# One ring of 1 MB weight units and fp32r products for the mixers of an eight-stage decoder kernel

## The chip, the cores and the metric

The kernel runs on one core of a Trainium2 chip. Its engines are TensorE (PE: matmuls; its weight loads are shown apart, as PEld), VectorE (DVE), ScalarE (ACT), GpSimd (POOL) and SyncE (SP), whose queue issues the weight loads. Each engine works through its own instructions in order and waits on semaphores. The metric is device time in microseconds, the median of several executions. One further execution is profiled; all rows come from that one.

## The reference, cut to what matters

256 tokens of width 1024 in float32 go through two blocks of two layers each: four mixers, three feed-forward networks, and a mixture of experts at the end.

```python
def first_block(x, ...):                      # layer 0: attention_mixer, layer 1: recurrent_mixer
    for layer in range(DEPTH):
        h = rmsnorm(x, norm_mix_pre[layer])
        m = attention_mixer(h, ...) if layer % 2 == 0 else recurrent_mixer(h, ...)
        x = x + rmsnorm(m, norm_mix_post[layer])
        h = rmsnorm(x, norm_ffn_pre[layer])
        f = swiglu(h, ffn_w_gate[layer], ffn_w_up[layer], ffn_w_down[layer])
        x = x + rmsnorm(f, norm_ffn_post[layer])

def second_block(x, ...):
    h = x + dilated_diff_mixer(rms_norm(x, attn_norm), attn_w_in, ..., attn_w_out)
    h = h + swiglu_2(rms_norm(h, ffn_norm), ffn_w_gate, ffn_w_up, ffn_w_down)
    h = h + hgrn2_mixer(rms_norm(h, hgrn_norm), hgrn_w_in, ..., hgrn_w_out)
    return h + moe_swiglu(rms_norm(h, moe_norm), moe_w_router, moe_w_gate, moe_w_up, moe_w_down)

def recurrent_mixer(h, w_in, conv_w, conv_b, w_a, b_a, w_i, b_i, lam, w_out):
    gate, xr = jnp.split(h @ w_in, 2, axis=-1)
    gate = jax.nn.gelu(gate, approximate=True)
    xc = causal_conv(xr, conv_w) + conv_b     # 4 taps, then blocks of 256 columns
    r = jax.nn.sigmoid(blocks(xc) @ w_a + b_a)
    i = jax.nn.sigmoid(blocks(xc) @ w_i + b_i)
    log_a = -LRU_C * r * jax.nn.softplus(-lam)
    a, u = jnp.exp(log_a), jnp.sqrt(-jnp.expm1(2.0 * log_a)) * i * xc
    hs = scan(a, u)                           # h_t = a_t h_(t-1) + u_t
    return (hs * gate) @ w_out

def swiglu(h, w_gate, w_up, w_down):          # d_ff 2816
    return (jax.nn.silu(h @ w_gate) * (h @ w_up)) @ w_down
```

The attention mixer (projection to 3072 columns) runs eight heads with a relative bias and eight with stick-breaking weights; the dilated mixer (3072 columns) normalises queries and keys per head and runs twelve dilated heads and four differential ones; the gated recurrence (4096 columns) works in chunks of 64 tokens with eight heads. Each ends with a product by a 1024x1024 output matrix. The mixture of experts has a router (top 2 of 8) and experts of d_ff 3584; the kernel streams the weights of all eight.

## The kernel before

All stages run one behind the other: mixer A (chunked and stick-breaking attention), network 0, mixer R (recurrent), network 1, mixer E (dilated and differential attention), network 2, mixer G (gated recurrence), experts M. Ahead of each stands a norm, behind each a residual.

**Weights** stream into a ring of slots of 2 MB, five of them up to the experts. `project` cuts a mixer's input matrix into loads of 512 columns, of which each gives two units: 256 columns for both halves of the tokens ("F", "H"), or 512 columns for one half ("T"). `project_out` makes two loads of 512 columns. Networks and experts load 1 MB at a time. SP issues the loads in a fixed order, each behind a wait for the slot's last reader.

**Products.** Mixers multiply in fp32 (`unit_tensor` L431, L435, L440; `out_tensor` L458): one matmul is two records in the trace. The networks use three fp32r products instead (`gate_up` L548 to L550, `down` L563 to L565): each weight half is split into a high half (ACT, `ffn_high` L518) and a low half (DVE, `ffn_low` L523, the raw minus the high), the activations likewise, and high·high, high·low and low·high are summed in PSUM. The experts do the same (L1691, L1696; matmuls L1700 to L1702).

**Norms.** ACT squares and sums a row half, GpSimd takes the root (`rstd`), DVE multiplies the token rows by it (L389), PE transposes (L410), and DVE multiplies each transposed tile by the norm weight as a per-partition column (L374). Ahead of a network ACT (L501) and DVE (L507) then split the result. `t` is the half of the tokens, so each step stands twice.

**In mixer R**, ACT evacuates each unit (L447), applies two sigmoids for each of eight gate tiles (L1101, L1102), which PE computes with the gate weights (L1082, from one 2 MB slot), then runs tanh (L1105), logarithm, exponentials (L1108 to L1111), the root (L1115) and three GELUs of the last units. DVE runs the convolution, the products between, the scan (L1147) and last the product by the gate (L1151), which the output projection reads. **In mixer E**, ACT takes a root for each unit of queries and keys (L1264), DVE a reciprocal and a product (L1322, L1324), and behind the last of these the scores get their bias (L1338). **In mixer G**, a chain of ACT and DVE steps runs for each of the first units, then a loop over the heads. **Ahead of the experts** DVE adds the last output projection (L485) and normalises, PE computes the router (L1726), and the first experts' units are split (L1691, L1696).

The order on each engine is as written in the functions of each stage (`R_scalar`, `R_vector`, `R_tensor` and so on); no scheduler moves it.

## Time and profile before

| | us |
|---|---|
| median of 3 executions | 2330.67 (2328.8 to 2332.07) |
| the profiled execution | 2333.04 |
| its span | 2331.3 |
| PE busy | 2191.8 (94%) |
| DVE busy | 1424.3 (61%) |
| ACT busy | 1194.4 (51%) |
| mean DMA rate | 229 GB/s |

The span is what the engines' first and last instructions enclose. The stages, by their first matmuls: A from 16.45, its projection from 148.25, network 0 from 187.89, R from 389.16 with its projection from 468.92, mixer G from 1101.64, the experts from about 1321.5. The chain that ended last is 84% PE, 8% ACT, 5% DVE. A busy share is a mean over stages with different limits, so it says little of any one of them; what ends an engine's idle time at a given place says more, and the rows below are chosen for that.

### The profile page before, as it was taken

The numbers are of one execution on the slowest core, as the hardware profiler recorded it, in microseconds if no ns is written. First come the engines' busy times: TensorE is split into PE (matmuls) and PEld (weight loads), VectorE is DVE, ScalarE is ACT, GpSimd is POOL, SyncE is SP. The second block draws the span as 40 slices with busy tenths as digits, with TensorE's granted clock in tenths as the row PEclk, the third lists the DMA queues.
The fourth block names the chain that finished last, engine by engine and source line by source line (L and its number), as shares of the span: only waits on it lengthen the run. The fifth ranks groups of instructions, "written<-read, shape, count | busy, mean of one in ns | idle before, by whom it ended". The sixth has DMA issues, their size and how long they took to land.

```text
span 2331.3 us, 28572 instructions
## 1 busy us (share of the span) xinstructions
PE 2191.8 (94%) x11126; PEld 1797.8 (77%) x11126; DVE 1424.3 (61%) x1256; ACT 1194.4 (51%) x1148; POOL 36.3 (2%) x87
## 2 busy tenths in 40 slices
PE   7988998979998978999897899999999999999998
PEld 5647997759997646998764588888888888888887
DVE  1335543345434364543424488889888888888888
ACT  1344431534332153432734267777677777776775
POOL 2000000000000000000000000000000000000000
PEclk9998998989998979999997799999999999999999
DMA  8305546434554303565420299999999999999997
GB/s 309 109 0 172 180 162 211 141 118 150 175 208 144 109 0 109 176 203 216 145 73 19 104 361 347 363 351 356 355 354 372 339 371 342 368 343 363 350 360 267
DMA packets 216998, 535.76 MB, mean 230 GB/s; under 512 B 9469, under 2 KB 79262, under 8 KB 216942
## 3 DMA queue, kind: packets, MB, share of 16 engines
q1 hardware_dynamic: 213936, 530.61, 63.4%
q0 software_dynamic: 1088, 4.19, 0.5%
q8 instruction: 39, 0.64, 0.1%
q10 hardware_dynamic: 1918, 0.18, 0.1%
q14 instruction: 17, 0.14, 0.0%
HBM read 533.90 MB, written 1.05 MB: 229 GB/s over the span
## 4 chain that ended last, share of the span: by engine, by line
PE 84%; ACT 8%; DVE 5%; issue 2%; POOL 0%; DMA 0%; ACTq 0%; DVEq 0%; POOLq 0%
PE ps L1700 12%; PE ps L1702 12%; PE ps L1701 11%; PE ps L431 8%; PE ps L548 6%; PE ps L549 6%; PE ps L550 6%; PE ps L458 5%; PE ps L435 3%; ACT ring_r L1691 3%; PE ps L563 3%; PE ps L564 3%; PE ps L565 3%; PE ps L1710 1%; PE ps L1753 1%
## 5 line engine op out<-in xcount | busy, mean ns | idle before, releaser
L1696 DVE TENSOR_TENSOR ring_r<-ring,ring_r 128x2048 fp32r<-128x2048 f32 x339 | 761.7, 2287 | 92.7 <-ACT ring_r L1691 92.7
L1691 ACT ACTIVATE ring_r<-ring 128x2048 fp32r<-128x2048 f32 x339 | 629.1, 1910 | 36.3 <-DMA ring<-in_moe_w_gate 29.3
L1700 PE MATMUL ps<-ring_r,arena_r 128*128 128x512 f32 x1344 | 531.8, 396 | 1.0 <-DVE arena_r L1932 1.0
L1702 PE MATMUL ps<-ring_r,arena_r 128*128 128x512 f32 x1344 | 524.4, 390 | 0.0
L1701 PE MATMUL ps<-ring_r,arena_r 128*128 128x512 f32 x1344 | 524.2, 390 | 0.0
L1702 PEld LDWEIGHTS ps<-ring_r,arena_r 128*128 128x128 f32 x1344 | 252.7, 188 | 54.6
L1700 PEld LDWEIGHTS ps<-ring_r,arena_r 128*128 128x128 f32 x1344 | 252.8, 188 | 51.5 <-issue 1.1
L1701 PEld LDWEIGHTS ps<-ring_r,arena_r 128*128 128x128 f32 x1344 | 253.1, 188 | 50.4
L431 PE MATMUL ps<-arena,ring 128*128 128x256 f32 x1152 | 259.6, 387 | 7.4 <-DVE arena L374 5.3
L431 PEld LDWEIGHTS ps<-arena,ring 128*128 128x128 f32 x1152 | 223.2, 194 | 43.3 <-DVE arena L374 6.6
L549 PE MATMUL ps<-arena_r,ring_r 128*128 128x256 f32 x816 | 233.4, 286 | 0.0
L550 PE MATMUL ps<-arena_r,ring_r 128*128 128x256 f32 x704 | 200.9, 285 | 0.0
L613 ACT ACTIVATE arena<-ps 128x256 f32<-128x256 f32 x66 | 25.3, 384 | 318.4 <-PE ps L550 318.4
L523 DVE TENSOR_TENSOR ring_r<-ring,ring_r 128x2048 fp32r<-128x2048 f32 x61 | 139.3, 2288 | 48.5 <-ACT ring_r L518 48.5
L548 PE MATMUL ps<-arena_r,ring_r 128*128 128x256 f32 x544 | 156.1, 287 | 4.9 <-DVE arena_r L507 4.9
L549 PEld LDWEIGHTS ps<-arena_r,ring_r 128*128 128x128 f32 x816 | 159.3, 195 | 1.2
L653 DVE TENSOR_TENSOR arena<-arena,ps 128x256 f32<-128x256 f32 x66 | 27.8, 422 | 190.7 <-ACT arena L613 190.7
L550 PEld LDWEIGHTS ps<-arena_r,ring_r 128*128 128x128 f32 x704 | 136.9, 194 | 0.0
L447 ACT ACTIVATE arena<-ps 128x512 f32<-128x512 f32 x44 | 25.9, 596 | 214.1 <-PE ps L431 149.1
L1840 ACT ACTIVATE arena_r<-ps 128x512 fp32r<-128x512 f32 x56 | 33.4, 597 | 176.1 <-PE ps L1753 176.1
L518 ACT ACTIVATE ring_r<-ring 128x2048 fp32r<-128x2048 f32 x61 | 115.9, 1904 | 9.3 <-DVE ring L1151 5.0
L523 DVE TENSOR_TENSOR ring_r<-ring,arena_r 128x2048 fp32r<-128x2048 f32 x38 | 87.1, 2293 | 53.0 <-ACT arena_r L518 53.0
(326 smaller groups left out, 2758.7 us busy)
## 6 DMA issues: line engine op xcount, KB each, us to landing
ring<-in_moe_w_gate SPq DMA_DIRECT2D x115, 1024.0 KB, 5.1
ring<-in_moe_w_up SPq DMA_DIRECT2D x112, 1024.0 KB, 5.1
ring<-in_moe_w_down SPq DMA_DIRECT2D x112, 1024.0 KB, 4.9
ring<-in_ffn_w_gate SPq DMA_DIRECT2D x33, 1024.0 KB, 7.3
ring<-in_ffn_w_up SPq DMA_DIRECT2D x33, 1024.0 KB, 9.7
ring<-in_ffn_w_down SPq DMA_DIRECT2D x33, 1024.0 KB, 5.0
ring<-in_attn_w_in SPq DMA_DIRECT2D x12, 2048.0 KB, 12.5
ring<-in_hgrn_w_in SPq DMA_DIRECT2D x8, 2048.0 KB, 9.8
```

Of the source, the lines that this page charges most:

```text
L431: mm = nc.tensor.matmul(bank[:, f * SEQ:(f + 1) * SEQ], w[:, kt, off + f * P:off + (f + 1) * P], HT[:, kt, :], start=(kt == 0), stop=(kt = ...
L458: mm = nc.tensor.matmul(Y[:, t, c * 512:(c + 1) * 512], actT[:, kt, t * P:(t + 1) * P], slot_k(plan[c][0])[:, kt, :], start=(kt == 0), sto ...
L518: nc.scalar.activation(high[h], w[:, h, :], ACT.Copy).then_inc(w_hi, 1)
L523: nc.vector.tensor_tensor(low[h], w[:, h, :], high[h], ALU.subtract).then_inc(w_lo, 1)
L548: nc.tensor.matmul(out_, wh[:, kt, c], f["HTh"][:, kt, :], start=(kt == 0), stop=False)
L549: nc.tensor.matmul(out_, wh[:, kt, c], HTl[:, kt, :], start=False, stop=False)
L550: mm = nc.tensor.matmul(out_, wl[:, kt, c], f["HTh"][:, kt, :], start=False, stop=(kt == KT - 1))
L1691: nc.scalar.activation(unit_parts(k)[0], ring[:, slot_of(k), 0:2048], ACT.Copy).then_inc(m_hi, 1)
L1696: nc.vector.tensor_tensor(low, ring[:, slot_of(k), 0:2048], high, ALU.subtract).then_inc(m_lo, 1)
L1700: nc.tensor.matmul(out_, x[:, 0, f, :], w[0], start=first, stop=False)
L1701: nc.tensor.matmul(out_, x[:, 1, f, :], w[0], start=False, stop=False)
L1702: return nc.tensor.matmul(out_, x[:, 0, f, :], w[1], start=False, stop=last)
```

## The change

The ring has five slots for units of 1 MB up to the experts; the halves of a slot hold the raw weights, which the low half overwrites, and the high half. Every stage takes its units in one order, `w_used` counts the units that PE is done with, and SP loads unit u when unit u−5 is counted. `highs_to` and `lows_to` issue splits, in order, up to a given unit, from wherever a stage's functions call them. Mixers' units (256 columns, always both token halves) and output projections (four units of 256 rows) are three fp32r products each; `out_high` and `out_low` split the activations of the projections. The norm weights come repeated over partitions (`gpre`) and multiply the token rows in two halves of 512 columns; the transposed result is split straight from PSUM. The networks' loop is written out, with d_ff in 11 pairs of tiles. The small rows' loads stand behind ACT's first three high halves.

On ACT, in mixer R, from its fifth unit on (`arena<-ps` L447 is a unit's evacuation, `ps,cols` the sigmoids). Before:

```order
L447 ACTIVATE ring<-ps 128x512 [waits s_unit]
L1101 ACT_TABLE_LOAD
L1101 ACTIVATE arena<-ps,cols 128x256 [waits r_gates]
L1102 ACTIVATE arena<-ps,cols 128x256
...
L1105 ACTIVATE ring<-arena,small 128x256 [waits r_sig]
L1105 ACTIVATE ring<-arena,small 128x256 x7
L1108 ACT_TABLE_LOAD
```

After:

```order
L464 ACTIVATE ring<-ps 128x512 [waits w_used]
L294 ACTIVATE ring_r_1_54<-ring 128x2048 [waits landed2]
L294 ACTIVATE ring_r_1_56<-ring 128x2048 [waits landed3]
L996 ACT_TABLE_LOAD
L996 ACTIVATE arena<-ps,cols 128x256 [waits r_gates]
...
L996 ACTIVATE arena<-ps,cols 128x256 [waits w_used]
L997 ACTIVATE arena<-ps,cols 128x256
L294 ACTIVATE ring_r_1_58<-ring 128x2048 [waits landed4]
L294 ACTIVATE ring_r_1_50<-ring 128x2048 [waits landed0]
L1001 ACTIVATE ring<-arena,small 128x256 [waits r_sig]
L1001 ACTIVATE ring<-arena,small 128x256 x7
```

Two high halves (L294) now stand ahead of the first sigmoid and two more between the last sigmoid and the first tanh (L1001).

On DVE, where the projections of mixer E end and the scores begin (`dist,ps` is the first of these). Before:

```order
L1322 RECIPROCAL ring<-ring 128x512 [waits e_rt]
L1324 SCALAR_TENSOR_TENSOR arena<-arena,cols,ring 128x512 [waits dve_step]
L1338 SCALAR_TENSOR_TENSOR arena<-dist,ps 128x384 [waits e_s,const_ok]
L1338 SCALAR_TENSOR_TENSOR arena<-dist,ps 128x384 [waits e_s] x2
```

After:

```order
L1223 RECIPROCAL ring<-ring 128x512 [waits e_rt]
L1225 SCALAR_TENSOR_TENSOR arena<-arena,cols,ring 128x512 [waits dve_step]
L303 TENSOR_TENSOR ring_r_0_49<-ring,ring_r_1_50 128x2048 [waits w_hi]
L303 TENSOR_TENSOR ring_r_0_51<-ring,ring_r_1_52 128x2048 [waits w_hi]
L303 TENSOR_TENSOR ring_r_0_53<-ring,ring_r_1_54 128x2048 [waits w_hi]
L1242 SCALAR_TENSOR_TENSOR arena<-dist,ps 128x384 [waits e_s,const_ok]
```

Three low halves (L303) have come between the last key product and the first biased scores.

On DVE ahead of the experts, from mixer G's last product to the transposed rows that the router reads. Before:

```order
L1618 TENSOR_TENSOR ring<-ring,arena 128x512 [waits s_evac,dve_step]
L1696 TENSOR_TENSOR ring_r_0_55<-ring,ring_r_1_56 128x2048 [waits m_hi]
L1696 TENSOR_TENSOR ring_r_0_57<-ring,ring_r_1_58 128x2048 [waits m_hi]
L1696 TENSOR_TENSOR ring_r_0_49<-ring,ring_r_1_50 128x2048 [waits m_hi]
L485 TENSOR_TENSOR arena<-arena,ps 128x1024 [waits s_y]
L389 TENSOR_SCALAR arena<-arena,rstd 128x1024 [waits s_rstd]
L485 TENSOR_TENSOR arena<-arena,ps 128x1024 [waits s_y]
L374 TENSOR_TENSOR arena<-ps,cols 128x4x128 [waits s_tr] x2
```

After:

```order
L1537 TENSOR_TENSOR arena<-arena 128x512 [waits s_evac,dve_step]
L477 TENSOR_TENSOR arena_r_66<-arena,arena_r_67 128x512 [waits s_oh] x4
L1613 TENSOR_TENSOR ring_r_0_49<-ring,ring_r_1_50 128x2048 [waits m_hi]
L1613 TENSOR_TENSOR ring_r_0_51<-ring,ring_r_1_52 128x2048 [waits m_hi]
L1613 TENSOR_TENSOR ring_r_0_53<-ring,ring_r_1_54 128x2048 [waits m_hi]
L375 TENSOR_TENSOR arena<-arena,ps 128x1024 [waits s_y]
L384 SCALAR_TENSOR_TENSOR arena<-arena,rstd,gpre 128x512 [waits s_rstd,gpre_in]
```

The three low halves of expert units stand ahead of the residual in both; what they wait for (`m_hi`, behind the landing in the slot) depends in the changed kernel on units of the output projection, which the last lines of the diff show.

The diff, cut to its core:

```diff
+        weights = []
+        split_no = []
+
+        def unit(shape, src, halves=True):
+
+            split_no.append(sum(n is not None for n in split_no) if halves else None)
+            weights.append((shape, src))
+            return len(weights) - 1
+
+        def columns_of(w, c0):
+            return unit(lambda v: v.rearrange("p (k n) -> p k n", k=KT), w.rearrange("(k p) n -> p k n", p=P)[:, :, c0:c0 + 256])
+
+        def rows_pair(w, r):
+            return unit(lambda v: v.rearrange("p (k n) -> p k n", k=2), w.rearrange("(k p) n -> p k n", p=P)[:, 2 * r:2 * r + 2, :])
+
+        slot_raw = lambda u: ring[:, u % NS_EARLY, 0:2048]
+        slot_lo = lambda u: ring_r[u % NS_EARLY][0][:, :]
+        slot_hi = lambda u: ring_r[u % NS_EARLY][1][:, :]
+        landed_at = lambda u: 16 * (u // NS_EARLY + 1)
+
+        evacs = [0]
 
...
+        def highs_to(act, last):
+
+            while high_done[0] <= min(last, N1 - 1):
+                u = high_done[0]
+                high_done[0] += 1
+                if split_no[u] is not None:
+                    act.wait_ge(landed[u % NS_EARLY], landed_at(u))
+                    nc.scalar.activation(slot_hi(u), slot_raw(u), ACT.Copy).then_inc(w_hi, 1)
+
+        def lows_to(dve, last):
+
+            while low_done[0] <= min(last, N1 - 1):
+                u = low_done[0]
+                low_done[0] += 1
+                if split_no[u] is not None:
+                    dve.wait_ge(w_hi, split_no[u] + 1)
+                    nc.vector.tensor_tensor(slot_lo(u), slot_raw(u), slot_hi(u), ALU.subtract).then_inc(w_lo, 1)
+
+        def weights_ready(pe, u):
+            pe.wait_ge(w_lo, split_no[u] + 1)
+
+        used = lambda u: (w_used, u + 1)
...
+        def by_columns(pe, u, bank, fs=(0, 1)):
+
+            wh, wl = (v.rearrange("p (k n) -> p k n", k=KT) for v in (slot_hi(u), slot_lo(u)))
+            for f in fs:
+                o = bank[:, f * SEQ:(f + 1) * SEQ].rearrange("p (t n) -> p t n", t=TT)
+                c = slice(f * P, f * P + P)
+                for kt in range(KT):
+                    nc.tensor.matmul(o, wh[:, kt, c], HTh[:, :, kt, :], start=(kt == 0), stop=False)
+                    nc.tensor.matmul(o, wh[:, kt, c], HTl[:, :, kt, :], start=False, stop=False)
+                    mm = nc.tensor.matmul(o, wl[:, kt, c], HTh[:, :, kt, :], start=False, stop=(kt == KT - 1))
+            return mm
...
         def unit_tensor(pe, plan, j, nbanks):
-            kind, s, n, off, tt, u = plan[j]
-            pe.wait_ge(landed[s], n)
+            kind, u, e = plan[j]
+            weights_ready(pe, u)
             if j >= nbanks:
-                pe.wait_ge(s_evac, u - nbanks + 1)
...
+                pe.wait_ge(s_evac, e - nbanks + 1)
+            (by_columns if kind == "F" else by_tokens)(pe, u, ps[:, j % nbanks, :]).then_inc(w_used, 1)
+
+        def unit_scalar(act, plan, j, nbanks, dst, func=ACT.Copy, scale=1.0):
+            act.wait_ge(*used(plan[j][1]))
...
+        def out_tensor(pe, plan, m, high, low):
+
+            for t in range(TT):
+                for n, (u, r) in enumerate(plan):
+                    if t == 0:
+                        weights_ready(pe, u)
+                        pe.wait_ge(s_ol, 4 * m + r + 1)
+                    wh, wl = (v.rearrange("p (k n) -> p k n", k=2) for v in (slot_hi(u), slot_lo(u)))
+                    for kt in range(2):
+                        xh, xl = (x[:, 2 * r + kt, t * P:(t + 1) * P] for x in (high, low))
+                        for c in range(2):
+                            o, cs = Y[:, t, c * 512:(c + 1) * 512], slice(c * 512, (c + 1) * 512)
+                            first, last = n == 0 and kt == 0, n == 3 and kt == 1
+                            nc.tensor.matmul(o, xh, wh[:, kt, cs], start=first, stop=False)
+                            nc.tensor.matmul(o, xl, wh[:, kt, cs], start=False, stop=False)
+                            mm = nc.tensor.matmul(o, xh, wl[:, kt, cs], start=False, stop=last)
+                    if t:
+                        mm.then_inc(w_used, 1)
+                if t == 0:
+                    mm.then_inc(s_y, 1)
...
+        def norm_turn(pe, k, t):
+
+            for h in range(2):
+                pe.wait_ge(s_xn, 4 * k + 2 * t + h + 1)
+                for kt in range(4):
+                    mm = nc.tensor.transpose(ps[:, 4 + 2 * t + h, kt * P:(kt + 1) * P],
+                                             XN[:, t, (4 * h + kt) * P:(4 * h + kt + 1) * P], ident[:, :])
+                mm.then_inc(s_tr, 1)
...
+        def normalise_tokens(dve, step, k, t):
+
+            c = 2 * k + t
+            dve.wait_ge(gpre_in, 16 * (k + 1))
+            dve.wait_ge(s_rstd, c + 1)
+            for h in range(2):
+                d = slice(512 * h, 512 * h + 512)
+                nc.vector.scalar_tensor_tensor(XN[:, t, d], X[:, t, d], rstd[:, c:c + 1], gpre[:, d],
+                                               ALU.mult, ALU.mult).then_inc(s_xn, 1)
...
+                highs_to(act, g[i] + ahead)
+                act.wait_ge(*used(g[i]))
+                if i >= 2:
+                    act.wait_ge(s_v, h0 + i - 1)
+                nc.scalar.activation(silu[:, i % 2, :], ps[:, 2 * (i % 2), :], ACT.Silu).then_inc(s_sg, 1)
+                highs_to(act, u[i] + ahead)
+                act.wait_ge(s_v, h0 + i + 1)
+                if i >= 2:
...
         def R_scalar(act, step):
...
+                highs_to(act, R_plan[j][1] + 3)
                 unit_scalar(act, R_plan, j, 2, R_x[:, 2 * j:2 * j + 2, TAPS:])
             gate = lambda j: unit_scalar(act, R_plan, j, 2, R_gate[:, 2 * (j - 4):2 * (j - 4) + 2, :], ACT.Gelu_apprx_tanh)
+            highs_to(act, R_plan[4][1] + 3)
             gate(4)
+            highs_to(act, R_plan[7][1])
...
+            highs_to(act, R_out[1][0])
             act.wait_ge(r_sig, KT)
             for j in range(KT):
                 ins = nc.scalar.activation(R_tau[:, j, :], R_r[:, j, :], ACT.Tanh, scale=decay_neg[:, j:j + 1])
...
             nc.scalar.activation(R_u, R_u, ACT.Sqrt, scale=2.0).then_inc(r_mult, 1)
             gate(6)
             gate(7)
-            act.wait_ge(r_out, 4)
-            first_split_scalar(act, FFN[1])
+            highs_to(act, R_out[3][0] + 1)
+            for q in range(4):
+                out_high(act, 1, q, (R_y, (r_out, q + 1)), R_oh)
...
+            lows_to(dve, R_out[3][0] + 1)
             for u in range(4):
-                dve.wait_ge(s_evac, R_plan[4 + u][5] + 1)
+                dve.wait_ge(s_evac, R_plan[4 + u][2] + 1)
                 nc.vector.tensor_tensor(R_y[:, 2 * u:2 * u + 2, :], R_h[:, 2 * u:2 * u + 2, :],
                                         R_gate[:, 2 * u:2 * u + 2, :], ALU.mult).then_inc(r_out, 1)
-            first_split_vector(dve, FFN[1])
+            for q in range(4):
+                out_low(dve, 1, q, R_y, R_oh, R_ol)
...
+            highs_to(act, E_out[3][0] + 1)
             exps(0)
...
+            lows_to(dve, E_plan[2][1])
             for i in range(8):
+                lows_to(dve, E_plan[E_F[i]][1] + 3)
                 normalise(i)
+            lows_to(dve, E_out[3][0] + 1)
             dve.wait_ge(const_ok, 2)
...
+                highs_to(act, G_plan[u][1] + 3)
                 unit_scalar(act, G_plan, u, 4, G_b[:, 2 * u:2 * u + 2, :])
                 act.wait_ge(g_na, u + 1)
                 step.link(nc.scalar.activation(G_ls[:, u, :], G_ls[:, u, :], ACT.Exp))
...
+                highs_to(act, G_plan[4 + u][1] + 3)
                 unit_scalar(act, G_plan, 4 + u, 4, G_q[:, 2 * u:2 * u + 2, :], ACT.Silu)
...
-                    sp.dma_start(dst, src).then_inc(landed[s], 16)
+            for u, (shape, src) in enumerate(weights):
+                if u >= NS_EARLY:
+                    sp.wait_ge(*used(u - NS_EARLY))
+                sp.dma_start(shape(slot_raw(u)), src).then_inc(landed[u % NS_EARLY], 16)
...
             for k in range(NU):
                 if k < NS_EARLY:
-                    sp.wait_ge(*freed[slot_of(k)])
+                    sp.wait_ge(*used(N1 - NS_EARLY + k))
                 elif k < NS:
-                    sp.wait_ge(s_y, 14)
+                    sp.wait_ge(*used(N1 - 1))
```

## Rows read from the trace of the kernel before

**Rows 1.** Stretches: us; busy (count) of PE, PEld, DVE, ACT, POOL; clock; DMA share; GB/s.
```profile
16.40:148.00 131.60, 118.32 (x496) 82.86 (x496) 39.18 (x93) 41.60 (x83) 4.98 (x12) 0.94 0.45 160
...
185.70:375.90 190.20, 188.03 (x1316) 177.50 (x1316) 89.24 (x78) 74.26 (x78) 0.00 (x0) 0.98 0.54 178
...
389.00:469.00 80.00, 72.10 (x321) 62.46 (x321) 27.79 (x49) 32.81 (x51) 0.00 (x0) 0.95 0.31 106
...
1321.50:2331.30 1009.80, 1001.45 (x4632) 830.09 (x4632) 865.49 (x502) 716.16 (x474) 0.00 (x0) 0.99 0.94 346
```

**Rows 2.** The chain that ended last: one fp32 unit, one fp32 output projection.
```profile
148.25 27.75 PE ps L458 x64
...
743.39 6.91 PE ps L431 x32
```

**Rows 3.** The timeline, PE: start, length as modelled, line (fp32r, 256 then 512 columns).
```profile
232.77 0.28 PE L550 MATMUL ps<-arena_r,ring_r 128*128 128x256 f32 x1
232.89 0.40 PE L563 MATMUL ps<-ring_r,arena_r 128*128 128x512 f32 x1
...
235.41 0.39 PE L565 MATMUL ps<-ring_r,arena_r 128*128 128x512 f32 x1
```

**Rows 4.** Stretches, columns as in rows 1: PE just after an idle stretch.
```profile
905.20:909.50 4.30, 4.28 (x20) 4.28 (x21) 3.16 (x2) 4.12 (x3) 0.00 (x0) 0.50 1.10 350
```

**Rows 5.** The page's costliest groups: the two halves of a weight split.
```profile
L518 ACT ACTIVATE ring_r<-ring 128x2048 fp32r<-128x2048 f32 x61 | 115.9, 1904 | 9.3 <-DVE ring L1151 5.0
L523 DVE TENSOR_TENSOR ring_r<-ring,arena_r 128x2048 fp32r<-128x2048 f32 x38 | 87.1, 2293 | 53.0 <-ACT arena_r L518 53.0
```

**Rows 6.** The page's DMA issues: KB each, median us from issue to landing.
```profile
ring<-in_ffn_w_down SPq DMA_DIRECT2D x33, 1024.0 KB, 5.0
...
ring<-in_rg_w_i SPq DMA_DIRECT2D x1, 1024.0 KB, 8.3
```

**Rows 7.** The timeline of the norm after the first output projection, ACT and PE.
```profile
176.03 1.02 ACT L465 ACTIVATE arena<-ps 128x1024 f32<-128x1024 f32 x1 [7.80 <-PE ps L458]
...
187.89 0.58 PE L548 MATMUL ps<-arena_r,ring_r 128*128 128x256 f32 x1 [2.17 <-DVE arena_r L507]
```

**Rows 8.** The timeline of the first attention, DVE, ACT and PE.
```profile
116.84 0.50 PE L869 MATMUL ps<-arena 64*128 64x128 f32 x4
...
120.42 1.76 DVE L1017 SCALAR_TENSOR_TENSOR ring<-arena 128x1536 f32<-128x1536 f32 x1
```

**Rows 9.** The timeline of the recurrent mixer, from its first unit on.
```profile
389.16 37.25 PE L431 MATMUL ps<-arena,ring 128*128 128x256 f32 x160 [0.79 <-DVE arena L374]
...
426.25 13.98 PE L1082 MATMUL ps<-arena,ring 128*128 128x256 f32 x64
...
441.13 3.31 ACT L1105 ACTIVATE ring<-arena,small 128x256 f32<-128x256 f32 x8
...
456.13 7.14 PE L431 MATMUL ps<-arena,ring 128*128 128x256 f32 x32 [2.10 <-ACT ring L447]
...
466.37 2.50 DVE L1151 TENSOR_TENSOR ring<-arena,ring 128x512 f32<-128x512 f32 x4
...
468.92 2.07 PE L458 MATMUL ps<-ring 128*128 128x512 f32 x2 [5.64 <-DVE ring L1151]
```

**Rows 10.** The timeline of the dilated attention, where its projections end.
```profile
802.04 0.60 ACT L447 ACTIVATE arena<-ps 128x512 f32<-128x512 f32 x1 [5.93 <-PE ps L440]
...
809.57 0.55 DVE L1338 SCALAR_TENSOR_TENSOR arena<-dist,ps 128x384 f32<-128x384 f32 x1 [1.81 <-PE ps L1211]
```

**Rows 11.** The timeline of the gated recurrence, first and ninth unit.
```profile
1101.64 28.54 PE L431 MATMUL ps<-arena,ring 128*128 128x256 f32 x131 [0.78 <-DVE arena L374]
...
1164.17 6.06 PE L435 MATMUL ps<-ring,arena 128*128 128x512 f32 x8 [7.01 <-ACT arena L447]
```

**Rows 12.** The timeline ahead of the experts, DVE and the router on PE.
```profile
1300.07 1.22 DVE L485 TENSOR_TENSOR arena<-arena,ps 128x1024 f32<-128x1024 f32 x1 [9.58 <-PE ps L458]
...
1306.31 7.00 PE L1726 MATMUL ps<-wrouter,arena 128*128 128x8 f32 x32 [0.94 <-DVE arena L374]
```

862 lines of the change are left out of this document (350 added, 512 removed).

## The prediction, written before the changed kernel had run

> **What bounds the kernel now.** I read first the stretches of the span. In the experts (1321.5 on) TensorE is busy 1001 of 1010 us at full clock, and in a feed-forward network 188 of 190 [rows 1]; neither leaves anything to another engine. The first mixer is different: 118 of 132 us, with ACT at 42 and DVE at 39. So what the change does to TensorE's work in mixers counts, and so does every wait that it puts between ACT, DVE and the transfers there. I then read the ends of idle times at each stage's borders, because these say which chain a mixer ends on.
>
> **What it removes.** Mixers and their output projections run in fp32 now: a unit of 256 weight columns takes 6.91 us, an output projection 27.75 [rows 2]. The changed kernel has three fp32r products for each, as the feed-forward networks do already. These start 0.12 us apart with 256 columns (232.77 to 232.89) and (235.41−232.89)/11 = 0.229 with 512 [rows 3]. A unit of 48 then takes 48×0.12 = 5.76, 1.15 less; an output projection 96×0.229 = 22.0, 5.75 less. With 48 units and 4 projections that is 55+23 = 78 us, 3.3% of the span, if all of it lay on the path and nothing came in its place. After an idle stretch TensorE is granted 0.50, 1.2 GHz: 20 matmuls in 4.30 us, where full clock takes 2.4 [rows 4], so each restart after a longer wait costs up to 2 us more; I count it where new waits arise.
>
> **What it adds.** Each 1 MB unit is split: 1.90 us on ACT, 2.29 on DVE [rows 5]. TensorE may begin a unit only behind both, and the next load of a slot waits for the unit five earlier. A load takes 5.0 us from issue to landing alone, and 8.3 when it is the second of a pair issued together [rows 6]. So where a split of a unit far ahead stands in ACT's or DVE's order ahead of the mixer's own work, a chain that began with a TensorE unit's end now begins 5.0+1.9+2.3 = 9.2 later. I price each stage with that.
>
> **First mixer.** Its 12 units save 13.8, of which I leave 8.4 where the next scores follow the last unit (116.84 before, 108.4 now [rows 8]), since units wait for splits that stand behind the bias and softplus work. But the end isn't set by units. DVE's stick-breaking work, whose last piece ran 1.76 from 120.42, now stands between splits of 2.29 each, and I get their last at 121.2 against 122.2. The two low halves of the mixer's output (activations are split too) cost 1.4 behind that. The output projection then starts 0.4 later, is 5.75 shorter: **−5.4**.
>
> **Norms.** From the first square behind the first output projection to the next matmul is 11.9 us [rows 7]. The two halves of the weight-multiplied rows, the transposes for each half and the split straight from PSUM drop the products of transposed tiles, of which two were on the chain, and start each step on a half: two and a half pieces of 0.63 (a DVE product of 128x512; four take the 2.50 further down), −1.65, and as much at the third norm. At the others DVE's first product waits for GpSimd's root ahead of the second residual, which takes most of that back: −0.2, −0.2, −0.4, +0.3. Together **−3.8**.
>
> **Feed-forward.** The same matmuls, so the price is only at the end: a split of 2.29 stands between DVE's last product and last low half, covered by one half of a down projection. I take **+3** for three, and 0 for the unrolled code.
>
> **Recurrent mixer** (starts at 389.16 [rows 9]). Five units take 31.1 for 37.25 (−6.1). ACT then waits for the landing of the unit nine ahead, in front of all sigmoids; its slot is freed by the last units, and TensorE's gate products wait for sigmoids from the third on. I get the gates' end at 53.1 from the start, 2.0 later than the 51.1 of before (426.25+13.98). Then comes the worst place: ACT splits the first two output units ahead of the tanh, and their slots are those of the gate weights, which are free only at the gates' end. 53.1+8.3+1.9 = 63.3, where the tanh started at 52.0 (441.13): +11.3, less up to 0.4 for the slot freed one product early: +10.9. Everything behind it (the chain of logarithm, exponentials, root, scan) moves with it. The last unit, 7.14 before, restarts at half clock: 5.76+2.2 = 8.0, +0.9. DVE's four last products (2.50, from 466.37) now stand behind the low half of the unit whose slot this unit frees. Its end, 456.13+10.9+8.0 = 475.0, plus 9.2, plus 2.5 and 0.7 for activations' low half: 487.4, where the projection started at 468.92: +18.5. Less 5.75: **+12.75**.
>
> **Dilated attention.** Here the units do lie on the path: −13.6. Before, the first biased scores came 7.53 behind the last evacuation's start (809.57−802.04 [rows 10]), and DVE had been idle for 1.81 by then: its last product of the key norm ended at 5.7. Now three low halves stand between: ACT's high of the last one ends at 5.0+1.9 = 6.9, DVE is at it from 5.7 to 5.7+3×2.3 = 12.6: +5.05. Low halves of activations +0.75, projection −5.75: **−13.55**.
>
> **Gated recurrence.** In the first loop each of three iterations has a low half (2.3) ahead of the gate chain, and the first evacuation comes 1.35 sooner: +5.55. The later units were already late behind ACT (the ninth waited 7.01 [rows 11]); now the next split's 1.9+2.3 stand ahead, against five units that are shorter: +3.6. The head loop has two highs and a landing in it, +8.4 less 4.6 by shorter units: +3.8. Low halves +0.75, projection −5.75: **+7.95**.
>
> **Ahead of the experts.** The first residual starts at 1300.07 and the router at 1306.31, 6.2 behind [rows 12]. DVE's three low halves of expert units stand ahead of that residual in both kernels, but before their slots had long been free; now the slot of the third is freed by the second output unit of the second row half, 5.5 ahead of the projection's end. Landing −0.4, high +1.5, low +3.8; then the residuals and the norm run one behind the other: the router starts at 15.7, **+9.5**. The experts themselves: **0**, since TensorE sets them.
>
> **Sum:** −5.4−3.8+3+12.75−13.55+7.95+9.5 = +10.45. The profiled execution took 2333.0 with a span of 2331.3, so the next would show a span near 2342. The median of before is 2330.67, 2.4 below its profiled execution; for the median I take 2330.67+10.4 = **2341**.
>
> A rule of the Trainium skill speaks to the largest term. Its page DMA: Bandwidth & Descriptors, under Anatomy of one DMA — SWDGE (gpsimd) path, puts the time of one transfer at about 2.0 us plus the bytes at 436 GB/s, an estimate of 4.4 us for 1 MB, where the trace has 5.0 [rows 6]. By the page each place where a landing is waited for would be 0.6 shorter, some 4 us over the seven, and the sum would be about +6.
>
> **Bounds of what no row shows.** How long a landing takes when five slots refill in a mixer: 5.0 to 8.3 [rows 6], at about seven places where something waits for it: 0 to +3.3 each; where loads queue singly I take 5.0, the row of such a load. How much of the first mixer's 13.8 arrives: from 0 to the 8.4 at its units' end, so −14 to −5. Extra ACT and DVE work inside mixers, 64 splits of 4.2 beside other work: 0 to +10. fp32r spacing with moving operands in two pieces of 128 columns, which the changed products have: no row has such a form; 0 to +10 ns each for 5472 matmuls is 0 to +55, and I take 0, since the products of [rows 3] run over as many columns.
>
> **Rivals.** (a) The waits are much shorter than priced, and the gain shows. For it: every hold is worked out from orders of issue, and a chain may be further behind than its split anyway. If the attention's chain follows its units (−8.4 in place of +0.4, so −9) and each of seven holds is 1 to 2 us shorter (−10), the time is 2341−19 = 2322. It decides from about 15 us less in holds. (b) It comes out even: holds 1 us shorter each, 2331 to 2334. (c) More work beside: DVE and ACT, not landings, become what mixers end on, since low halves stand ahead of every evacuation's successor; +10 on the forecast, 2351. (d) The two-piece moving operand costs 10 ns each: +55, 2396; its point is the start distance, 0.13 in place of 0.12. (e) The change doesn't do what it says, that is fp32 products weren't the price: a unit as long as before, +55 on the forecast; nothing speaks for it, as the networks' products show 0.12. I put it with (d).
>
> **How the numbers follow.** A measurement of this kernel can tell about 0.2%, 4.7 us, from no change. The forecast, with its own range from 2335.5 to 2350, gets 0.50. (a) 0.20; (b) 0.15; (c) 0.10; (d) with (e) 0.05. Faster by over 0.2% 0.21, within 0.2% 0.18, slower 0.61. The range has to leave out at most 2 in 10: I leave out (d) and the far half of (a), and take 2321 to 2356.
>
> **What would show it.** A unit's matmuls end 5.8 after their first, output projections 22.0. Between the last sigmoid and the first tanh stand 9 to 10 us in which ACT waits for a landing; the recurrent mixer's projection starts 97 to 99 behind its first unit. DVE goes from the last key norm product through three low halves to the biased scores. The router starts 15 behind the gated recurrence's last projection matmul, not 6. The experts take 1010. I am wrong if ACT isn't held ahead of the tanh, if the first mixer's last stick-breaking sum comes 8 sooner, or if starts of the products in mixers are over 0.125 apart.

## The result and the profile after

| | before | after |
|---|---|---|
| median, us | 2330.67 (2328.8 to 2332.07, 5 executions) | 2341.84 (2341.47 to 2342.81, 5 executions) |
| profiled execution | 2333.04 | 2342.1 |
| its span | 2331.3 | 2340.4 |
| ratio after to before | | 1.0048, 95% interval 1.0033 to 1.0063 |

The changed kernel is 0.5% slower, by 11.2 us in the medians and 9.1 in the spans of the two profiled executions. The forecast was 2341, between 2321 and 2356.

The page of the profile after, its busy times and the groups that answer to units and splits:

```profile
PE 2128.1 (91%) x12182; PEld 1852.7 (79%) x12182; DVE 1566.5 (67%) x1281; ACT 1325.9 (57%) x1194; POOL 39.1 (2%) x94
...
L436 PE MATMUL ps<-arena_r,ring_r 128*128 128x256 f32 x1632 | 477.0, 292 | 49.8 <-DVE ring_r L303 29.5
L303 DVE TENSOR_TENSOR ring_r<-ring,ring_r 128x2048 fp32r<-128x2048 f32 x163 | 371.4, 2288 | 90.0 <-ACT ring_r L294 89.9
L294 ACT ACTIVATE ring_r<-ring 128x2048 fp32r<-128x2048 f32 x163 | 309.6, 1905 | 79.4 <-DMA ring<-in_ffn_w_gate 56.2
```

TensorE is busy for 2128.1 us in place of 2191.8: 64 less, so the matmuls got shorter. That is less than the 78 of the prediction's sum; the mean granted clock of the span also fell, from 0.959 to 0.944, so part of the difference may be work at 1.2 GHz, but it wasn't split up. DVE has 1566.5 for 1424.3 and ACT 1325.9 for 1194.4. The rows name what TensorE and DVE now wait for: each unit's first product sat idle for 49.8 us in all, mostly for a low half (L303), a low half for 90.0 for its high half (L294), and a high half for 79.4, mostly for a transfer.

Where the time went is read from the first and last matmuls of each stage (a mixer from its first unit to its projection's first matmul; the projection to its last matmul's end; the four networks' and mixers' norms between). The sums on the right are those of the prediction.

| stage, us | before | after | change | forecast |
|---|---|---|---|---|
| start to first unit | 16.45 | 20.45 | +4.00 | 0 |
| first mixer | 131.80 | 131.77 | −0.03 | +0.4 |
| its projection | 27.73 | 22.01 | −5.72 | −5.75 |
| norms 1 to 6 | 62.97 | 60.66 | −2.31 | −3.8 |
| three networks | 567.10 | 569.65 | +2.55 | +3 |
| recurrent mixer | 79.76 | 98.31 | +18.55 | +18.5 |
| its projection | 29.58 | 23.68 | −5.90 | −5.75 |
| dilated mixer | 156.01 | 148.26 | −7.75 | −7.8 |
| its projection | 30.24 | 24.20 | −6.04 | −5.75 |
| gated recurrence | 168.22 | 175.59 | +7.37 | +13.7 |
| its projection | 30.17 | 24.84 | −5.33 | −5.75 |
| projection's end to router | 6.28 | 15.96 | +9.68 | +9.5 |
| router to the end | 1024.99 | 1025.02 | +0.03 | 0 |
| sum | | | +9.1 | +10.5 |

Three stages tell the story. **In the recurrent mixer**, on ACT, DVE, SP and PE (start, length, instruction, idle time ahead of it and who ended that):

```profile
442.21 0.47 ACT L997 ACTIVATE arena<-ps,cols 128x256 f32<-128x256 f32 x1
...
445.80 1.91 ACT L294 ACTIVATE ring_r<-ring 128x2048 fp32r<-128x2048 f32 x1 [3.12 <-DMA ring<-in_rg_w_out]
...
448.35 1.92 ACT L294 ACTIVATE ring_r<-ring 128x2048 fp32r<-128x2048 f32 x1 [0.63 <-DMA ring<-in_rg_w_out]
...
450.17 3.29 ACT L1001 ACTIVATE ring<-arena,small 128x256 f32<-128x256 f32 x8
```

The last sigmoid is done at 442.7, and the tanh, which has all that it reads, begins at 450.17: ACT waited for two transfers (3.12 and 0.63) and split them. Before, these steps were 0.02 apart ([rows 9], where the tanh starts at 441.13 behind a sigmoid that ends there). Further down the same mixer:

```profile
472.53 0.37 SPq L1923 DMA_DIRECT2D ring<-in_ffn_w_gate  x1
...
477.75 1.91 ACT L294 ACTIVATE ring_r<-ring 128x2048 fp32r<-128x2048 f32 x1 [1.01 <-DMA ring<-in_ffn_w_gate]
...
479.79 2.29 DVE L303 TENSOR_TENSOR ring_r<-ring,ring_r 128x2048 fp32r<-128x2048 f32 x1
...
482.00 2.49 DVE L1052 TENSOR_TENSOR ring<-arena,ring 128x512 f32<-128x512 f32 x4
...
485.24 0.77 PE L493 MATMUL ps<-ring_r,arena_r 128*128 128x512 f32 x1 [12.73 <-DVE ring_r L477]
```

The last unit ends at 472.5, SP loads the slot that it leaves, ACT's high half follows the landing at 477.75, DVE's low half at 479.79, and only then come the four products which the projection reads. TensorE was idle for 12.73 us ahead of the projection, against 5.64 before.

**In the dilated mixer**, DVE's rows where the projections end, which answer to [rows 10]:

```profile
804.51 0.75 DVE L1225 SCALAR_TENSOR_TENSOR arena<-arena,cols,ring 128x512 f32<-128x512 f32 x1
805.18 6.69 DVE L303 TENSOR_TENSOR ring_r<-ring,ring_r 128x2048 fp32r<-128x2048 f32 x3
811.79 1.01 DVE L1242 SCALAR_TENSOR_TENSOR arena<-dist,ps 128x384 f32<-128x384 f32 x2
```

Three low halves take 6.69 us between the last key product and the first scores. The biased scores come 12.3 behind the last unit's end (799.51), where they came 7.6 behind it. **Ahead of the experts**, against [rows 12]:

```profile
1291.29 5.81 SPq L1938 DMA_DIRECT2D ring<-in_moe_w_gate  x3
...
1298.25 2.29 DVE L1613 TENSOR_TENSOR ring_r<-ring,ring_r 128x2048 fp32r<-128x2048 f32 x1 [19.64 <-ACT ring_r L1608]
...
1299.13 1.91 ACT L1608 ACTIVATE ring_r<-ring 128x2048 fp32r<-128x2048 f32 x1 [0.91 <-DMA ring<-in_moe_w_gate]
...
1301.07 2.29 DVE L1613 TENSOR_TENSOR ring_r<-ring,ring_r 128x2048 fp32r<-128x2048 f32 x1 [0.53 <-ACT ring_r L1608]
...
1303.28 1.21 DVE L375 TENSOR_TENSOR arena<-arena,ps 128x1024 f32<-128x1024 f32 x1
...
1315.38 7.00 PE L1645 MATMUL ps<-wrouter,arena 128*128 128x8 f32 x32 [1.09 <-DVE arena L1802]
```

The first residual starts at 1303.28, 3.9 behind the projection's last matmul. The prediction calls the residual at 1300.07 of the kernel before the first one. It isn't: in the trace before, the first of the two residuals stands at 1286.33, under the second half of the projection, and the one at 1300.07 in [rows 12] is the second. More of that under the experiments.

### The profile page after: what moved, and what is told of

The parts are those of the page before. It is cut to its first block, busy times and chain, and to the rows that moved or that the text cites. A ratio compares the mean times of both kernels' runs of the same rounds, so it can differ in the third digit from the quotient of the medians.

```text
span 2340.4 us, 30214 instructions
## 1 busy us (share of the span) xinstructions
PE 2128.1 (91%) x12182; PEld 1852.7 (79%) x12182; DVE 1566.5 (67%) x1281; ACT 1325.9 (57%) x1194; POOL 39.1 (2%) x94
## 4 chain that ended last, share of the span: by engine, by line
PE 79%; ACT 9%; DVE 8%; issue 2%; DMA 1%; POOL 1%; DVEq 0%; ACTq 0%; POOLq 0%
PE ps L1617 12%; PE ps L1619 11%; PE ps L1618 11%; PE ps L436 8%; PE ps L437 8%; PE ps L438 8%; ACT ring_r L1608 3%; PE ps L516 2%; PE ps L517 2%; PE ps L518 2%; DVE ring_r L303 2%; PE ps L1627 1%; PE ps L493 1%; PE ps L494 1%; PE ps L495 1%
## 5 line engine op out<-in xcount | busy, mean ns | idle before, releaser
L1613 DVE TENSOR_TENSOR ring_r<-ring,ring_r 128x2048 fp32r<-128x2048 f32 x339 | 762.1, 2287 | 113.4 <-ACT ring_r L1608 113.2
L1608 ACT ACTIVATE ring_r<-ring 128x2048 fp32r<-128x2048 f32 x339 | 629.5, 1910 | 64.2 <-DMA ring<-in_moe_w_gate 51.8
L1617 PE MATMUL ps<-ring_r,arena_r 128*128 128x512 f32 x1344 | 531.8, 396 | 1.0 <-DVE arena_r L1856 1.0
L1619 PE MATMUL ps<-ring_r,arena_r 128*128 128x512 f32 x1344 | 524.4, 390 | 0.0
L1618 PE MATMUL ps<-ring_r,arena_r 128*128 128x512 f32 x1344 | 524.2, 390 | 0.0
L436 PE MATMUL ps<-arena_r,ring_r 128*128 128x256 f32 x1632 | 477.0, 292 | 49.8 <-DVE ring_r L303 29.5
L437 PE MATMUL ps<-arena_r,ring_r 128*128 128x256 f32 x1632 | 472.2, 289 | 0.0
L438 PE MATMUL ps<-arena_r,ring_r 128*128 128x256 f32 x1632 | 471.7, 289 | 0.0
L303 DVE TENSOR_TENSOR ring_r<-ring,ring_r 128x2048 fp32r<-128x2048 f32 x163 | 371.4, 2288 | 90.0 <-ACT ring_r L294 89.9
L436 PEld LDWEIGHTS ps<-arena_r,ring_r 128*128 128x128 f32 x1632 | 324.6, 199 | 56.5 <-DVE ring_r L303 25.2
L294 ACT ACTIVATE ring_r<-ring 128x2048 fp32r<-128x2048 f32 x163 | 309.6, 1905 | 79.4 <-DMA ring<-in_ffn_w_gate 56.2
L437 PEld LDWEIGHTS ps<-arena_r,ring_r 128*128 128x128 f32 x1632 | 324.7, 199 | 2.0 <-issue 1.0
L438 PEld LDWEIGHTS ps<-arena_r,ring_r 128*128 128x128 f32 x1632 | 324.0, 199 | 0.0
L1617 PEld LDWEIGHTS ps<-ring_r,arena_r 128*128 128x128 f32 x1344 | 252.8, 188 | 51.5 <-issue 1.2
L581 DVE TENSOR_TENSOR arena<-arena,ps 128x512 f32<-128x512 f32 x33 | 22.7, 688 | 237.8 <-PE ps L438 237.8
L516 PE MATMUL ps<-ring_r,arena_r 128*128 128x512 f32 x264 | 103.4, 392 | 3.0 <-DVE arena_r L584 3.0
L517 PE MATMUL ps<-ring_r,arena_r 128*128 128x512 f32 x264 | 103.1, 390 | 0.0
L518 PE MATMUL ps<-ring_r,arena_r 128*128 128x512 f32 x264 | 102.7, 389 | 0.0
L569 ACT ACTIVATE arena_r<-arena 128x512 fp32r<-128x512 f32 x33 | 20.9, 632 | 137.1 <-DVE arena L581 137.1
```

What stands on the lines that cost most here:

```text
L294: nc.scalar.activation(slot_hi(u), slot_raw(u), ACT.Copy).then_inc(w_hi, 1)
L303: nc.vector.tensor_tensor(slot_lo(u), slot_raw(u), slot_hi(u), ALU.subtract).then_inc(w_lo, 1)
L436: nc.tensor.matmul(o, wh[:, kt, c], HTh[:, :, kt, :], start=(kt == 0), stop=False)
L437: nc.tensor.matmul(o, wh[:, kt, c], HTl[:, :, kt, :], start=False, stop=False)
L438: mm = nc.tensor.matmul(o, wl[:, kt, c], HTh[:, :, kt, :], start=False, stop=(kt == KT - 1))
L516: nc.tensor.matmul(o, xh, wh[:, f, cs], start=(first and f == 0), stop=False)
```

## The experiments

All start from the changed kernel and move splits: the same instructions in another order, except in the run with longer units. Each was one execution with a profile, beside the kernel before on the same chip, and is read by its span (2340.4 for the changed kernel) and by its stages; only the two kernels at the end of this section that join the moves were timed with several executions. Medians of different chips differ by some 2 us, and single executions of the kernel before lay between 2326.9 and 2333.2, so a difference in span under 3 us is read from the stage alone. The changed kernel itself wasn't run again on the chips of these runs, so its one profile is the measure; where another run on the same chip has the same instructions in a stage, that one is given as a second measure.

**The tanh freed.**

```diff
-            highs_to(act, R_out[1][0])
             act.wait_ge(r_sig, KT)
...
             nc.scalar.activation(R_u, R_u, ACT.Sqrt, scale=2.0).then_inc(r_mult, 1)
+            highs_to(act, R_out[1][0])
             gate(6)
...
-            lows_to(dve, R_out[1][0])
             dve.wait_ge(r_inv, 1)
```

> Changed kernel, recurrent mixer only: ACT's two high halves that stood between the last sigmoid and the first tanh stand behind the root, DVE's two low halves behind the scan. The same work, no wait taken out of the program, only moved. Theory (a hold at a landing): the tanh starts right behind the last sigmoid, 7.5 us sooner than at 63.2 from the mixer's first unit, and so does everything to the scan's end. The output projection gains less, because five low halves of 2.29 now follow the scan in place of three: from 98.3 behind the first unit to 95.5, and the time falls by about 3 us. Rival (the extra work on ACT and DVE, not the wait, is what costs): the tanh starts earlier by no more than the two splits' 3.8 us, and the projection starts no earlier.

Span 2337.2, 3.2 less; the mixer 93.45 in place of 98.31, its projection 1.0 longer. ACT and DVE in its trace:

```profile
440.71 0.47 ACT L997 ACTIVATE arena<-ps,cols 128x256 f32<-128x256 f32 x1
441.21 3.31 ACT L1000 ACTIVATE ring<-arena,small 128x256 f32<-128x256 f32 x8
...
466.46 11.10 DVE L303 TENSOR_TENSOR ring_r<-ring,ring_r 128x2048 fp32r<-128x2048 f32 x5
477.48 2.49 DVE L1051 TENSOR_TENSOR ring<-arena,ring 128x512 f32<-128x512 f32 x4
```

The tanh follows the sigmoid at once, 54.0 behind the first unit (387.26) in place of 63.2: 9.3 sooner, by far more than the splits' own 3.8. The second measure is the run further down that only moves the third expert unit's split, on the same chip and with the changed kernel's recurrent mixer: its tanh starts 61.4 behind the first unit and its projection 97.5, so the tanh is 7.4 sooner (7.5 expected) and the mixer 4.0 shorter. Then DVE does five low halves, 11.1 us, between the scan and the last products, and about half of it is lost again. So the wait for the landing did hold the tanh, and a second cost stood behind it.

**Both places of the recurrent mixer freed.** DVE's part, beside the edit above; ACT's high half of the first network unit moves behind the activations' high halves as well:

```diff
-            lows_to(dve, R_out[3][0] + 1)
             for u in range(4):
                 dve.wait_ge(s_evac, R_plan[4 + u][2] + 1)
...
+            lows_to(dve, R_out[0][0])
             for q in range(4):
                 out_low(dve, 1, q, R_y, R_oh, R_ol)
+            lows_to(dve, R_out[3][0] + 1)
```

> As the kernel with the tanh freed, and DVE's last four products in the recurrent mixer ahead of the low halves, the first of which comes before the activations' low halves, the others behind; ACT's high half of the first network unit behind the activations' high halves. Theory: both holds are gone, the projection starts about 86.5 behind the first unit in place of 98.3, and the time falls by 11 to 12 us. Rival (work, not waits): the same splits have to be done before the projection ends, so that its end gains at most 3.

Span 2328.3, 12.1 less. The mixer takes 84.55, 13.8 less (12.9 by the second measure), its projection 24.06, so that the whole gain is there at the projection's end too: the rival of work, not waits, is out for this mixer. What is left against the 79.76 of before is 1.9 in the gate loop (the last sigmoid starts 53.4 behind the first unit, before 51.5) and about 3 for one low half and the first of the activations'.

**A longer hold at the same place.**

```diff
-            highs_to(act, R_out[1][0])
+            highs_to(act, R_out[2][0])
             act.wait_ge(r_sig, KT)
```

> Changed kernel, recurrent mixer: ACT waits ahead of the tanh for one output unit more (the third), whose slot only the sixth projection unit frees, some 6 us behind the gates. Theory (the landing sets the tanh): the tanh starts 4 us later, at 67.3 from the first unit, and projection and time move by the same 4. Rival (something else, such as the chain of sigmoids or DVE's product, sets the tanh): at most the 1.9 of one more high half.

Span 2344.6, 4.2 more. ACT's rows:

```profile
441.24 0.47 ACT L997 ACTIVATE arena<-ps,cols 128x256 f32<-128x256 f32 x1
...
451.55 1.91 ACT L294 ACTIVATE ring_r<-ring 128x2048 fp32r<-128x2048 f32 x1 [2.15 <-DMA ring<-in_rg_w_out]
453.36 3.28 ACT L1001 ACTIVATE ring<-arena,small 128x256 f32<-128x256 f32 x8
```

From the last sigmoid's start to the tanh it is 12.1 us in place of 8.0, the 4 expected. Counted from the first unit the tanh is only 2.3 later (65.6, not the expected 67.3), and the mixer 3.2 longer, since the sigmoids themselves ended 1.8 sooner in this execution, as in the two above. Against the second measure the tanh is 4.2 later and the projection 4.0. The two measures differ by the clock at the mixer's start. Four to six us behind the first unit, the changed kernel's trace and that of the second measure show (columns as in rows 1):

```profile
391.00:393.00 2.00, 2.00 (x11) 2.00 (x11) 2.00 (x2) 0.00 (x0) 0.00 (x0) 0.50 0.00 0
```

```profile
391.70:393.70 2.00, 2.00 (x19) 2.00 (x19) 2.00 (x2) 0.00 (x0) 0.00 (x0) 1.00 0.00 0
```

The first gate product comes 31.6 behind the first unit in the one, 30.4 in the other. So the changed kernel's own profile has nearly 2 us in this mixer that other executions of the same instructions don't have, 1.2 of them at 1.2 GHz in the first units.

**The third expert unit's split behind the last norm.**

```diff
-            for k in range(AHEAD):
+            for k in range(AHEAD - 1):
                 split_low(dve, 0, k)
             for t in range(TT):
                 residual(dve, step, 7, t)
...
+            split_low(dve, 0, AHEAD - 1)
```

ACT's `split_high` moves likewise.

> Changed kernel, ahead of the experts: only the third expert unit's high half (ACT) and low half (DVE) are moved behind the last norm. Theory: the first residual starts at once when the projection's first row half is complete, and the router starts 6.4 us behind the projection's last matmul in place of 16.0; the time falls by 9.5. Rival (the new norm, with its two halves and the waits for the root, is the longer chain): the router still starts 12 or more behind.

Missed: the router came 13.36 behind the projection in place of 15.96, a gain of 2.6 (span 2337.8), not 9.5. So the third split wasn't the whole hold. In its trace:

```profile
1296.08 1.92 ACT L1608 ACTIVATE ring_r<-ring 128x2048 fp32r<-128x2048 f32 x1 [18.77 <-DMA ring<-in_moe_w_gate]
...
1298.03 2.29 DVE L1613 TENSOR_TENSOR ring_r<-ring,ring_r 128x2048 fp32r<-128x2048 f32 x1 [18.39 <-ACT ring_r L1608]
1300.24 1.21 DVE L375 TENSOR_TENSOR arena<-arena,ps 128x1024 f32<-128x1024 f32 x1
```

The second split is late as well: its slot too comes free only in the projection's second half (SP issues three loads from 1290.86), its high half waits for the landing, and the residual starts behind its low half at 1300.24, though the first row half was complete some 12 us earlier.

**The second one too.** `range(1)` in place of `range(AHEAD - 1)`, and the other two behind the norm.

> As the router run, but the second expert unit's high and low half are moved behind the last norm too, as its landing (5.2 us behind its issue at 1291) held the first residual to the projection's end in that run. Theory (every landing ahead of the residual has to go; the first row half then is normalised under the second half of the projection): the first residual starts about 12 us ahead of the projection's last matmul, the router 6.5 behind it in place of 13.4, and the span falls by 9 against the changed kernel, 2331.4 in place of 2337.8. Rival (the new norm is the longer chain by itself): the router starts 10 or more behind.

Span 2332.4, 8.0 less than the changed kernel. The router follows at 7.36 behind the projection. DVE:

```profile
1288.84 1.22 DVE L375 TENSOR_TENSOR arena<-arena,ps 128x1024 f32<-128x1024 f32 x1 [8.51 <-PE ps L495]
...
1299.73 1.22 DVE L375 TENSOR_TENSOR arena<-arena,ps 128x1024 f32<-128x1024 f32 x1 [6.00 <-PE ps L495]
```

The first residual and its norm now run 11 us ahead of the projection's end (1299.7), as before the change. What the change had cost here is the overlap of the first row half's norm with the second half's projection. Both landings had to go: moving the third split alone gave 2.6, moving the second as well another 6.0.

**Low halves behind the dilated mixer's attention.** `lows_to(dve, E_out[3][0] + 1)` moves from ahead of the first biased scores to the end of the mixer.

> Changed kernel, dilated attention: only DVE's three low halves ahead of the first biased scores are moved to the mixer's end. Theory: the biased scores start 7.6 us behind the last projection matmul in place of 12.3, and the time falls by 4.7. Rival (ACT's high half, which waits for the landing, holds the scores' exponentials): the biased scores come sooner but the projection starts as late as before, 0 to 1.

Span 2336.4, 4.0 less; the mixer 143.55 in place of 148.26, 4.7 less, and the biased scores (806.67) are 7.6 behind the last unit's end again, as before the change. Three other runs on this chip leave this mixer as it is, and it takes 148.2 to 148.3 in each.

**The gated recurrence's first loop.**

```diff
-                lows_to(dve, G_plan[u][1] + 3)
+                if not u:
+                    lows_to(dve, G_plan[u][1] + 3)
                 ls, mx, ad = G_ls[:, u, :], G_mx[:, u, :], G_ad[:, u, :]
                 dve.wait_ge(s_evac, G_evac(u))
                 nc.vector.scalar_tensor_tensor(ls, f2, -1.0, f2, ALU.mult, ALU.min).then_inc(g_na, 1)
+                lows_to(dve, G_plan[u][1] + 3)
```

On ACT the high half moves behind the evacuation in the same way.

> Changed kernel, gated recurrence, first loop: the low half stands behind DVE's first product of each turn, where DVE waits for ACT, and the high half behind the evacuation. Theory: a turn takes 13.6 us in place of 15.7, the chain ends 6.3 sooner and so does the mixer. Rival (the later units set the mixer's end): the chain ends sooner, the mixer by at most 1.

Span 2334.5, 5.9 less, the mixer 168.80 in place of 175.59. Two turns on DVE, the changed kernel first:

```profile
1121.58 2.26 DVE L303 TENSOR_TENSOR ring_r<-ring,ring_r 128x2048 fp32r<-128x2048 f32 x1
1123.77 0.68 DVE L1449 SCALAR_TENSOR_TENSOR ring<-arena 128x512 f32<-128x512 f32 x1
...
1137.29 2.27 DVE L303 TENSOR_TENSOR ring_r<-ring,ring_r 128x2048 fp32r<-128x2048 f32 x1
```

```profile
1122.48 0.67 DVE L1452 SCALAR_TENSOR_TENSOR ring<-arena 128x512 f32<-128x512 f32 x1
1123.06 2.28 DVE L303 TENSOR_TENSOR ring_r<-ring,ring_r 128x2048 fp32r<-128x2048 f32 x1
1125.79 0.69 DVE L1456 SCALAR_TENSOR_TENSOR ring<-arena,ring 128x512 f32<-128x512 f32 x1 [0.44 <-ACT ring L1379]
...
1135.99 0.67 DVE L1452 SCALAR_TENSOR_TENSOR ring<-arena 128x512 f32<-128x512 f32 x1
```

A turn was 15.7 us with the low half ahead of its first product and is 13.5 with it behind, where it fills an idle stretch; 0.44 of waiting is left there.

**The first mixer's low halves** around the stick-breaking sums move behind the second sums, ACT's high half of the first network unit behind the last copies.

> Changed kernel, first mixer: DVE's low halves around the first stick-breaking sums are moved behind the second, and ACT's high half of the first network unit behind the last copies. Theory (low halves hold the stick-breaking chain, and ACT a landing of its own): the output projection starts 3.5 to 6 us sooner than 152.2, most likely 5. Rival (the chain is late because the mixer starts 4.0 late, at 20.45): at most 1.

The projection starts at 145.09, 7.1 sooner, more than the best of the range. But 1.9 of it is there already at the mixer's first stick-breaking scores (95.92 for 97.78), ahead of anything that moved; from there on it is 5.3, within the range. The rival, a chain that is late because the mixer starts late, is out. The projection takes 23.6 in place of 22.0, and the span is 2334.9, 5.5 less. Two stretches show why the projection is longer (as in rows 1), the first of this kernel, the second of the changed one:

```profile
145.00:147.00 2.00, 1.91 (x5) 1.56 (x6) 2.00 (x4) 0.78 (x2) 0.00 (x0) 0.55 0.00 0
```

```profile
152.20:154.00 1.80, 1.78 (x8) 1.51 (x9) 1.68 (x3) 0.71 (x2) 0.00 (x0) 1.00 0.00 0
```

TensorE was idle for 3.61 us ahead of it here, since a high half of 1.9 us now stands ahead of the activations' own, and it starts at 0.55, near 1.2 GHz; behind 1.81 us it had 2.4 GHz. A wait taken away at one place can move one to another place, and its price is then the clock.

**The start.** The loads of the bias and the post-norm weights stand behind GpSimd's first roots, and ACT splits the first unit ahead of the activations' halves.

> Changed kernel, start only: the loads of the relative bias and of the first post-norm weights are issued behind GpSimd's first roots, and ACT splits the first unit ahead of the activations' high halves. Theory: the repeated norm weights land sooner than 11.0 and the first unit starts near 17 in place of 20.45; the first mixer ends 3.5 sooner. Rival (the first unit's own landing sets the start): 0 to 1.5.

The first unit starts at 17.76, 2.7 sooner, and the projection at 151.70, 0.5 sooner; the span is 2339.8. The start is shorter nearly as expected, but the 3.5 expected at the mixer's end didn't come: the mixer doesn't end on its start, but on the stick-breaking chain, which the run before this one moved.

**Longer units.**

```diff
                     nc.tensor.matmul(o, wh[:, kt, c], HTl[:, :, kt, :], start=False, stop=False)
+                    if again:
+                        nc.tensor.matmul(o, wl[:, kt, c], HTh[:, :, kt, :], start=False, stop=False)
```

The units whose weights are the moving operand get the same. `again` is set for mixers only.

> Changed kernel with 16 matmuls of 256 columns more in each of the mixers' 48 units (the product of the low weights is added twice, so the units' sums are a little off), 1.92 us each, 92 in all; waits and splits are as in the changed kernel. It tells how much of a unit's length lies on the path in each mixer. Theory (as the prediction's sum has it): the recurrent mixer is 11.5 longer (its first five units and its last), the dilated one 23 (all twelve), the first about 15 (its stick-breaking chain has 8 us of cover), the gated recurrence 15 to 17; 66 in all, a span near 2406. Rival (holds set the mixers' ends, units hardly count): under 30 in all, 2370.

Span 2410.2, 69.8 more (66 expected). The first mixer is 15.07 longer, the recurrent one 10.89, the dilated one 24.33, the gated recurrence 18.51 (its projection and the others within 1.3). So of each microsecond of a unit about three quarters are on the path, and unevenly so: all in the dilated mixer, not quite six of eight units in the recurrent one. In the first mixer 8 us of the 23 are covered, and ahead of the stick-breaking chain: its first scores are already 14.8 later (112.59 for 97.78), its projection 14.8 too. That this mixer's shorter units brought nothing has another cause, the splits in that chain (next section).

**All moves together**, and then **with the norms' order** changed too (ahead of the recurrent mixer, the dilated mixer and the gated recurrence, DVE adds the second residual before it normalises the first row half):

```diff
+            if k in (2, 4, 6):
+                residual(dve, step, k, 1)
             normalise_tokens(dve, step, k, 0)
-            if k:
+            if k and k not in (2, 4, 6):
                 residual(dve, step, k, 1)
             normalise_tokens(dve, step, k, 1)
```

> The changed kernel with all moves of splits together: recurrent mixer (both places), second and third expert unit, dilated mixer's low halves, gated recurrence's first loop, first mixer's low halves, and the start. All work is there. Theory (the gain of the products was lost in holds, and these are apart from each other): the singles add up, 12.1+9+4.0+5.9+5.5+0.6 = 37, a span of 2303 and a median near 2305, 1.1% below the kernel before. Rival (freed places meet the next hold, or DVE and ACT as such): half of that, 2320 or more.

> As all2, and in the norms ahead of the recurrent mixer, the dilated mixer and the gated recurrence DVE adds the second residual ahead of the first row half's norm. Theory (DVE's product waits for GpSimd's root ahead of work that is ready): each of these norms 0.5 to 1.5 shorter, 1.5 to 4 in all, 2302. Rival (the order only changes which half is late): within 0.5 of all2.

| us | before | all moves | with the norms' order |
|---|---|---|---|
| median | 2332.32 | 2306.75 | 2298.49 |
| ratio to before | | 0.9903 (0.9889 to 0.9918) | 0.9862 (0.9847 to 0.9878) |
| span of the profiled execution | | 2304.6 | 2302.1 |
| recurrent mixer | 79.76 | 84.09 | 85.53 |
| norms 2 and 4, together | 23.83 | 24.74 | 20.77 |
| gated recurrence | 168.22 | 168.98 | 168.92 |
| projection's end to router | 6.28 | 7.35 | 7.35 |

(The column before has the median of the runs on the same chip, and the stages of its own profile above.) The joined moves give 35.8 us in the span, where the singles give 12.1+8.0+4.0+5.9+5.5+0.6 = 36.1: they add up, and the rival of a next hold is out. With the same work, splits and ring as the changed kernel, 1.0% below the kernel before. The order in the norms gives 4.0 us in two norms, of which the profile shows 2.5 in the span; the medians are 8.3 apart, but the profiled execution of the last kernel was its slowest, 2303.9 where the three others were 2298.2 to 2298.7. What these 5 us are is not shown: no profile was taken of one of the three. The version with everything is the fastest here, 1.4% below the kernel before.

## Why the prediction was right, point by point

**What bounds it, and the gain of the products.** TensorE's share of busy time fell as said, units take 48 starts 0.12 apart, projections are 5.3 to 6.0 shorter for the 5.75 of the sum. Rival (d), a price of the moving operand in two pieces, and (e) are out: TensorE's starts in the mixers are 0.12 apart like those of [rows 3], here in the gated recurrence:

```profile
1110.97 0.28 PE L436 MATMUL ps<-arena_r,ring_r 128*128 128x256 f32 x1
...
1111.34 0.28 PE L436 MATMUL ps<-arena_r,ring_r 128*128 128x256 f32 x1
```

None of the three signs of being wrong came: ACT was held, the starts are 0.12 apart, and the first mixer's last stick-breaking sum came 2.3 sooner (134.90 for 137.17), not 8. Rivals (a) and (b), shorter waits throughout, don't fit the two largest holds, which came at their price (+18.55 and +9.68). Of (c), more work beside, the mechanism is there: low halves that wait for no transfer cost 4.7 in the dilated mixer, 5.3 in the first and 6.8 in the gated recurrence. The sum had priced it in two of the three and too small in the first mixer.

**First mixer: the total missed by 3.65.** The projection starts at 152.22, 4.0 later than before, where the sum had 0.4. The first unit also starts 4.0 later, by a chain that the prediction didn't put in at all:

```profile
11.01 3.05 DVE L384 SCALAR_TENSOR_TENSOR arena<-arena,rstd,gpre 128x512 f32<-128x512 f32 x4 [8.95 <-DMA gpre<-in_norm_mix_pre]
...
20.45 0.55 PE L436 MATMUL ps<-arena_r,ring_r 128*128 128x256 f32 x1 [4.90 <-DVE ring_r L303]
```

DVE waits for the repeated norm weights until 11.01 (the transposes began at 9.10 before), ACT splits the first unit behind all the activations' halves, and DVE follows. But the start isn't shown to be the cause, and the equal 4.0 looks like chance. In the eight traces that have this mixer unchanged its first unit starts between 19.14 and 20.52 and its projection between 151.83 and 153.25, and the earliest start has the latest projection; and the run with a start 2.7 sooner moved the projection by 0.5.

That the stick-breaking chain, not the units, sets the end was right. The step that failed is the piece of it for which the prediction had an end of 121.2, 1.0 sooner than before. It ended at 125.03 (123.27+1.76), 3.8 later than that. ACT's and DVE's rows, and of the kernel before the sum alone:

```profile
104.99 1.49 ACT L810 ACTIVATE arena<-arena 128x1536 f32<-128x1536 f32 x1
106.39 1.90 ACT L294 ACTIVATE ring_r<-ring 128x2048 fp32r<-128x2048 f32 x1
...
108.31 2.29 DVE L303 TENSOR_TENSOR ring_r<-ring,ring_r 128x2048 fp32r<-128x2048 f32 x1 [6.15 <-ACT ring_r L294]
110.52 1.75 DVE L901 SCALAR_TENSOR_TENSOR arena<-ring,arena 128x1536 f32<-128x1536 f32 x1
...
117.72 2.28 DVE L303 TENSOR_TENSOR ring_r<-ring,ring_r 128x2048 fp32r<-128x2048 f32 x1
...
123.27 1.76 DVE L896 SCALAR_TENSOR_TENSOR arena<-arena 128x1536 f32<-128x1536 f32 x1
```

```profile
109.71 1.76 DVE L1023 SCALAR_TENSOR_TENSOR ring<-arena,ring 128x1536 f32<-128x1536 f32 x1 [4.34 <-ACT ring L944]
```

The logarithm (L810) ends at 106.48, and the sum (L901) starts at 110.52. A high half and a low half stand between, 4.0 us, where before the sum followed the logarithm at once. A second low half costs 2.3 ahead of the next scores. Up to the first scores the mixer was 3.2 sooner than before (97.78 for 100.98), and these two places took more than that. From the last of these pieces to the projection it is 28.95 for 27.83, +1.1 for the 1.4 taken.

**Norms, −2.31 for −3.8.** Norms 1 and 3 gained 1.5 each as said (1.65); those ahead of the recurrent and the dilated mixer lost 0.45 each, where −0.2 was taken. DVE's product waits there for GpSimd's root with the second residual ready behind it, which the last run shows to cost 2.0 each. **Networks, +2.55 for +3**: right as a sum; it wasn't tested apart.

**Recurrent mixer, +18.55 for +18.5.** The end is right to 0.1, the steps less so. The tanh starts 63.2 behind the first unit for 62.9 to 63.3, but the sigmoids end 3.8 later than before, not 2.0, and the pair of landings took 4.8 and 6.5 from issue, not the 8.3 of [rows 6] for its second. So only 7.5 us lie between the last sigmoid and the tanh, not the 9 to 10 of the prediction, and ACT waits in 3.75 of them. The last unit took 7.35, not 8.0. Each of these was off by about 2 or less and they cancelled. The 2.0 of the sigmoids was right for the runs with full clock sooner (1.9); in the two of them with this mixer unchanged its total is +17.7 and +18.1.

**Dilated mixer, −7.75 for −7.8.** The three low halves stand where the sum had them, and the run without them gives back 4.7 of the 5.05.

**Gated recurrence, +7.37 for +13.7.** The first loop was dearer than taken, the later part nearly free. The chain's end is 69.8 behind the first unit, before 62.5 (1164.14−1101.64): +7.3 for +5.55, since each of three turns is 2.2 longer as taken, and the first evacuation is 0.65 later, not 1.35 sooner. That is the clock: in the first 4 us of this mixer TensorE had 1.2 GHz behind the new norm, and 2.4 before the change (last section). From the chain's end to the projection it is 105.80 for 105.72. The prediction had +8.15 there: 3.6 for later units, 3.8 for the head loop, 0.75 for low halves. The two highs and the landing that it put into the head loop (+8.4) are the term that was most wrong. Up to ACT's first copy in that loop the change is +1.7, for +3.6; through the loop, to its last output, it is −2.3, for +3.8. The prediction counted the highs as if ACT had nothing to wait for there. In the trace none of the loop's four highs waits for a landing, and behind each of the first three ACT still waits for TensorE's unit, 3.84, 1.44 and 1.41 us; the first:

```profile
1214.04 0.60 ACT L464 ACTIVATE arena<-ps 128x512 f32<-128x512 f32 x1 [3.84 <-PE ps L438]
```

No run moved these highs, so this is read from the trace alone. The longer units cost 18.5 in this mixer, 9.6 units' worth, so the gain that the sum took from shorter ones (11.7, ten units' worth) was about right.

**Ahead of the experts, +9.68 for +9.5.** The size is right, and the price of the place, but the cause was told too simply: it named the third unit's slot alone, and freeing that gave 2.6. Two landings hold the residual, and what is lost is the overlap with the projection's second half. The sum came out because it counted both residuals and the norm behind the last low half, as the trace has them.

**The sum.** 9.1 in the spans for 10.45; the misses are +3.65, +1.5, −0.45, −0.1, −0.25, −5.9 and +0.2. The two large ones had opposite signs, so that the median's agreement to 1 us is luck by some 4 us. Without the first of them the median would be 2338.2, without the second 2347.7; both lie within the forecast's own range, 2335.5 to 2350. That the medians are 11.2 apart and the spans 9.1 is the kernel before: its profiled execution was 2.4 above its median.

**The Trainium skill's price of a load**, weighed in the prediction (its page DMA: Bandwidth & Descriptors, under Anatomy of one DMA — SWDGE (gpsimd) path, gives an estimate of 4.4 us for 1 MB, the trace of before 5.0), doesn't decide anything here. The page's figure is for transfers on GpSimd's path, and the weights here go through SP's queue. The trace of after has 4.8 to 5.6 as medians for the weights, above the estimate (loads that share the queue are among them), so the price of the row was the better one.

## What to carry to other kernels

A split, copy or prefetch that waits for a transfer holds everything behind it on its in-order engine; ask of each one which slot it needs, who frees that slot and when, and put it where the engine would wait anyway. The same instructions in another order were worth 36 us here, nearly half of the 78 that the faster matmuls could give. And a gain in TensorE's work has to be priced stage by stage: lengthening the work on purpose tells quickly how much of it lies on the path.

## What the runs showed of the hardware

A restart's clock depends on more than the idle time just ahead of it. At the gated recurrence's first unit, before and after the change (columns as in rows 1):

```profile
1101.60:1103.60 2.00, 1.96 (x9) 1.75 (x10) 0.00 (x0) 0.00 (x0) 0.00 (x0) 1.00 1.05 386
```

```profile
1098.90:1101.00 2.10, 2.01 (x9) 2.01 (x10) 0.99 (x2) 2.10 (x2) 0.00 (x0) 0.50 0.33 123
```

TensorE's idle time just ahead is 0.78 and 1.41 us, and it had 2.4 GHz in one and 1.2 in the other, behind norms of 7.3 and 7.5 us with the same 16 transposes. The length of that idle time alone doesn't tell them apart: the first mixer's projection started behind 1.81 us at a granted clock of 1.00 (152.20 to 154.00 above), behind attention products and not behind a norm. In the gated recurrence the evacuation of the first unit comes 7.9 us behind the unit's start for 7.2 before, though its matmuls at full clock are 1.15 shorter.

The two kinds of records don't always agree: in the changed kernel's first 4 us the matmuls start 0.21 apart, as at 1.2 GHz (20.80, 21.02, 21.23), while the stretch 20.40 to 22.40 shows a granted clock of 1.00.
